# Scheduling edits across a hybrid GLA / sliding-window / gated-DeltaNet trunk on one core

## The reference, cut to what matters

```
x <- LN(ALPHA * x + even_mixer(x))     # GLA heads and sliding-window attention, one output projection
x <- LN(ALPHA * x + swiglu(x))         # 1024 -> 2816 -> 1024
x <- LN(ALPHA * x + gated_delta(x))    # conv(4) + SiLU on q, k, v; chunks of 64; inverse of (I + A)
x <- LN(ALPHA * x + swiglu(x))
GLA:   attn = where(causal, q_g @ k_g.T, 0) per chunk of 64; o = attn @ v + q_g @ state
delta: tmat = inverse(I + tril(kb @ k.T * gam, -1)); u = tmat @ vb; w = tmat @ (kb * exp(decay))
       v_new = u - w @ state; o = qd @ state + (q @ k.T * gam) @ v_new
       out = rms_norm(o) * norm_g * silu(gate)
```

## Time and profile before

| | us |
|---|---|
| median of 3 runs (1284.8 to 1287.28) | 1285.05 |
| the profiled execution | 1283.91 |
| its span, first to last instruction | 1282.1 |
| TensorE busy | 1250.3 (98%) |
| GpSimd busy | 598.9 (47%) |
| VectorE busy | 462.7 (36%) |
| ScalarE busy | 432.9 (34%) |

### The profile page before, as it was taken

The page is one execution under the profiler, slowest core; times in us unless marked ns, Lnnn a source line. Parts: engine busy times, 40 slices in busy tenths (PEclk is TensorE's granted clock), DMA queues, the critical chain, the costliest instruction groups (busy, mean ns, idle before and its releaser), DMA issues.

```text
span 1282.1 us, 16970 instructions
## 1 busy us (share of the span) xinstructions
PE 1250.3 (98%) x7104; PEld 1027.5 (80%) x7104; DVE 462.7 (36%) x763; ACT 432.9 (34%) x600; POOL 598.9 (47%) x286
## 2 busy tenths in 40 slices
PE   9999999999999999998999999999999999999997
PEld 7878877888888888886777878887788888888885
DVE  5548945211111000115687955553521101010105
ACT  4174623322222221224453355452422222221111
POOL 4241243964444443445743346364595444435341
PEclk9999999999999999999999999999999999999999
DMA  9321032333333233231344342022233333324221
GB/s 305 99 67 66 1 115 84 99 99 99 98 99 99 83 121 125 99 96 49 98 110 124 99 100 92 26 67 99 66 99 99 99 99 99 99 82 134 80 99 65
DMA packets 109375, 122.98 MB, mean 96 GB/s; under 512 B 22386, under 2 KB 84148, under 8 KB 109300
## 3 DMA queue, kind: packets, MB, share of 16 engines
q1 hardware_dynamic: 101828, 118.59, 29.4%
q10 hardware_dynamic: 7472, 3.31, 1.0%
HBM read 117.96 MB, written 3.70 MB: 95 GB/s over the span
## 4 chain that ended last, share of the span: by engine, by line
PE 86%; DVE 7%; POOL 3%; issue 3%; DVEq 1%; ACT 1%; ACTq 0%; POOLq 0%
PE bank L1562 26%; PE bank L1563 26%; PE bank L1564 26%; PE bank L1893 3%; POOL w_lo L638 2%; DVE f_ab L1083 1%; DVE KH L1355 1%; DVE OO L1333 1%; DVE SS L1331 1%; PE bank L1608 1%; DVEq L435 1%; PE bank L1721 0%; PE bank L1845 0%; DVE x_tm L1106 0%; PE bank L1782 0%
## 5 line engine op out<-in xcount | busy, mean ns | idle before, releaser
L638 POOL TENSOR_TENSOR w_lo<-w_raw,w_hi 128x1024 fp32r<-128x1024 f32 (+1 forms) x200 | 470.0, 2374 | 495.3 <-ACT w_hi L768 495.3
L1562 PE MATMUL bank<-x_hi,w_hi 128*128 128x512 f32 x928 | 364.3, 393 | 7.5 <-DVE f_ab L1083 4.0
L1564 PE MATMUL bank<-x_hi,w_lo 128*128 128x512 f32 x928 | 361.7, 390 | 0.0
L1563 PE MATMUL bank<-x_lo,w_hi 128*128 128x512 f32 x928 | 361.6, 390 | 0.0
L768 ACT ACTIVATE w_hi<-w_raw 128x1024 fp32r<-128x1024 f32 (+1 forms) x200 | 196.3, 1031 | 218.3 <-issue 167.3
L1562 PEld LDWEIGHTS bank<-x_hi,w_hi 128*128 128x128 f32 x928 | 174.6, 188 | 46.9 <-issue 8.4
L1564 PEld LDWEIGHTS bank<-x_hi,w_lo 128*128 128x128 f32 x928 | 174.5, 188 | 36.6
L1563 PEld LDWEIGHTS bank<-x_lo,w_hi 128*128 128x128 f32 x928 | 174.5, 188 | 35.4
L1150 DVE TENSOR_TENSOR f_ab<-bank,f_ab 128x512 f32<-128x512 f32 x44 | 30.4, 691 | 368.9 <-PE bank L1564 368.9
L1563 PE MATMUL bank<-w_lo,h_hi 128*128 128x512 f32 x352 | 140.4, 399 | 0.0
L1562 PE MATMUL bank<-w_hi,h_hi 128*128 128x512 f32 x352 | 138.7, 394 | 0.0
(11 more groups left out here) (270 smaller groups left out, 1179.5 us busy)
## 6 DMA issues: line engine op xcount, KB each, us to landing
w_raw<-ffn_w_gate_dram SPq DMA_DIRECT2D x22, 1024.0 KB, 5.3
w_raw<-ffn_w_up_dram SPq DMA_DIRECT2D x22, 1024.0 KB, 5.3
w_raw<-ffn_w_down_dram SPq DMA_DIRECT2D x20, 1024.0 KB, 5.0
w_raw<-od_w_in_dram SPq DMA_DIRECT2D x16, 1024.0 KB, 5.9
w_raw<-ev_w_in_dram SPq DMA_DIRECT2D x8, 1024.0 KB, 5.9
w_raw<-ev_w_out_dram SPq DMA_DIRECT2D x4, 1024.0 KB, 5.1
w_raw<-od_w_out_dram SPq DMA_DIRECT2D x4, 1024.0 KB, 5.1
x_fm<-x_fm_dram SPq DMA_DIRECT2D x8, 256.0 KB, 6.7
```

Of the source, the lines that this page charges most:

```text
L638: pool.tensor_tensor(w_lo[:, b % 2, c], w_raw[:, b % 2, c], w_hi[:, b % 2, c].bitcast(F32), ALU.subtract).then_inc(w_lo_ready, 1)
L1562: pe.matmul(out_ap, st[0], mv_[0], start=start, stop=False)
L1563: pe.matmul(out_ap, st[0], mv_[1], start=False, stop=False)
L1564: return pe.matmul(out_ap, st[1], mv_[0], start=False, stop=stop)
```

## The change

The masked GLA products are done by 64 x 64 chunk blocks instead of 128 x 128. Tail and last fillers are reordered by halves of k, and ("mix", 0, 0, 2) becomes a filler. LayerNorm's normalisation is written in two halves, each with its own z_norm count; GpSimd waits for all of them before it subtracts the first half of the next weight block, which now stands ahead of its low parts of x. fm_block with fresh does the two products with x_hi before it waits for x_lo. Bank rings restart in other places and orders. The inverse blocks lie in DRAM as two whole arrays, written by whole rows and read by two DMAs in place of one. The copy of ba_fm moves from VectorE to ScalarE, and ScalarE's rounding of the first og blocks moves ahead of two SiLUs. In the chunk loop qk stands between the small product and the small blocks, and filler place 0 ahead of vTM. The last tile's scale and gate are one VectorE instruction a head. Left out below: the shapes of g_at and upto (64 columns instead of 128) and three waits on blocks_landed, 128 instead of 64 a tile.

```diff
@@ -78,8 +78,7 @@
...
     i = np.arange(P)
-    same = (i[:, None] // CH) == (i[None, :] // CH)
-    upto = (same & (i[:, None] <= i[None, :])).astype(np.float32)
+    upto = (i[:, None] % CH <= np.arange(CH)[None, :]).astype(np.float32)
@@ -164,8 +163,10 @@
...
+EVEN_FILLERS = [[("gr", t)] for t in range(NT)]
 TAIL_FILLERS = {0: [("mix", 0, 0, 0), ("mix", 0, 0, 1)], 1: [("mix", 1, 0, 2)]}
-FILLED = set(FILLERS.values()) | set(TAIL_FILLERS[0]) | set(TAIL_FILLERS[1])
+LAST_FILLERS = {0: [("mix", 0, 0, 2)], 1: []}
+FILLED = set(FILLERS.values()) | set(TAIL_FILLERS[0] + TAIL_FILLERS[1] + LAST_FILLERS[0])
@@ -189,11 +190,12 @@
...
     for t in tiles:
-        u += [("score", t, 0), ("score", t, 1), ("kd", t), ("gr", t), ("gattn", t), ("gstate", t, 0), ("gout", t),
-              ("gstate", t, 1), ("probT", t, 0), ("probT", t, 1), ("sout", t)]
+        u += [("score", t, 0), ("score", t, 1), ("kd", t)] + EVEN_FILLERS[t]
+        u += [("gattn", t), ("gstate", t, 0), ("gout", t), ("gstate", t, 1), ("probT", t, 0), ("probT", t, 1)]
...
             u += [("oT", 0, t - 1, 0), ("oT", 0, t - 1, 1)]
-    u += TAIL_FILLERS[0] + [("oT", 0, NT - 1, 0), ("oT", 0, NT - 1, 1)]
+        u += [("sout", t)]
+    u += TAIL_FILLERS[0] + [("oT", 0, NT - 1, 0), ("oT", 0, NT - 1, 1)] + LAST_FILLERS[0]
@@ -220,9 +222,9 @@
...
         if t == 0:
-            u += filler(-1) + gram + both("kTM", "vTM") + filler(0) + both("qk") + filler(1) + m1 + filler(2) + ds
+            u += filler(-1) + gram + both("kTM") + filler(0) + both("vTM", "qk") + filler(1) + m1 + filler(2) + ds
         else:
-            u += gram + both("kTM", "vTM") + m1 + ds + both("qk") + filler(1) + both("kS")
+            u += gram + both("kTM", "vTM") + m1 + both("qk") + ds + filler(1) + both("kS")
@@ -235,12 +237,15 @@
...
     for key in u:
-        if key == ("conv", CONV_ORDER[0]):
+        if key == ("ba_fm",):
...
         elif key == FILLERS[0, -1]:
-            ring, turn = [0, 1, 2, 3, 6, 7, 4, 5], 0
+            ring, turn = [0, 6, 7, 1, 2, 3, 4, 5], 0
+        elif key == TAIL_FILLERS[1][0]:
+            free = [slots[k][0] for k in (("ds", NT - 1, 64), ("oT", 1, NT - 2, 0), ("oT", 1, NT - 2, 1))]
+            ring, turn = free + [b for b in ring if b not in free], 0
@@ -401,7 +406,7 @@
...
         dec32_dram = nc.dram_tensor("dec_rows32_out", (P // SB, TH, SB), F32).ap()
-        t_dram = nc.dram_tensor("t_blocks", (P, SB, 2, SB), F32).ap()
+        t_dram = nc.dram_tensor("t_blocks", (2, P, SB, SB), F32).ap()
@@ -596,9 +601,9 @@
...
             sp.wait_ge(s["t_blk_ready"], 1)
-            sp.dma_start(t_dram[:, :, 1, :], t_blkT).then_inc(s["t_blk_out"], 16)
+            sp.dma_start(t_dram[1, :, :, :], t_blkT).then_inc(s["t_blk_out"], 16)
             sp.wait_ge(s["t_blk_ready"], 2)
-            sp.dma_start(t_dram[:, :, 0, :], t_blk).then_inc(s["t_blk_out"], 16)
+            sp.dma_start(t_dram[0, :, :, :], t_blk).then_inc(s["t_blk_out"], 16)
@@ -607,8 +612,9 @@
...
                 for q in range(P // SB):
-                    src = t_dram[q * SB + t * GDN_H:q * SB + (t + 1) * GDN_H, :, :, :].rearrange("h i a c -> i h a c")
-                    sp.dma_start(blocks_in[q * SB:(q + 1) * SB, :, :, :], src).then_inc(s["blocks_landed"], 16)
+                    for a in range(2):
+                        src = t_dram[a, q * SB + t * GDN_H:q * SB + (t + 1) * GDN_H, :, :].rearrange("h i c -> i h c")
+                        sp.dma_start(blocks_in[q * SB:(q + 1) * SB, :, a, :], src).then_inc(s["blocks_landed"], 16)
@@ -632,8 +638,10 @@
...
         def _(pool):
-            def split_lo(b):
+            def split_lo(b, part=(0, 1)):
                 for i, c in enumerate(pieces(b)):
+                    if i not in part:
+                        continue
@@ -718,18 +726,18 @@
...
                             split_lo(first_block[name] + 1)
-                gate_output(NT - 1)
...
                     continue
-                split_lo(b)
+                split_lo(b, (1,) if b - 1 in turned else (0, 1))
...
                 if b in turned:
+                    pool.wait_ge(s["z_norm"], 2 * NT * turned[b])
+                    split_lo(b + 1, (0,))
@@ -878,8 +886,10 @@
...
                     act.activation(s_p[:, g, :], s_p[:, g, :], ACT.Exp).then_inc(s["s_prob"], 1)
-                full(act, ("gr", t))
-                take(act.activation(g_r[:, t, :], bank(("gr", t))[:, :], ACT.Silu), ("gr", t))
+                for key in EVEN_FILLERS[t]:
+                    if key[0] == "gr":
+                        full(act, key)
+                        take(act.activation(g_r[:, key[1], :], bank(key)[:, :], ACT.Silu), key)
@@ -923,6 +933,11 @@
...
                                scale=convw[:, 9 * KD + n:9 * KD + n + 1]).then_inc(s["conv_raw"], 1)
+                if i == 1:
+                    full(act, ("ba_fm",))
+                    take(act.activation(ba_fm[:, :], bank(("ba_fm",))[:, :], ACT.Copy), ("ba_fm",))
+                if i == len(CONV_ORDER) - 1:
+                    split_to(first_block[("og", 0)] + 1)
@@ -973,7 +988,6 @@
...
                     act.activation(decay32, decay32, ACT.Exp).then_inc(s["exp32"], 1)
-            split_to(first_block[("og", 0)] + 1)
@@ -1111,8 +1125,10 @@
...
                         return
-                    dve.tensor_scalar(x_tm[:, t, :], x_tm[:, t, :], mv[:, t, 0:1], rstd[:, t:t + 1],
-                                      ALU.subtract, ALU.mult).then_inc(s["z_norm"], 1)
+                    for h in range(2):
+                        c = slice(h * 512, (h + 1) * 512)
+                        dve.tensor_scalar(x_tm[:, t, c], x_tm[:, t, c], mv[:, t, 0:1], rstd[:, t:t + 1],
+                                          ALU.subtract, ALU.mult).then_inc(s["z_norm"], 1)
@@ -1250,8 +1266,11 @@
...
                 full(dve, ("gattn", t))
-                take(dve.copy_predicated(g_at[:, :, :], over_heads(upto[:, :].bitcast(I32), GH), k4(("gattn", t))),
-                     ("gattn", t))
+                take(dve.copy_predicated(g_at[:, :, :], over_heads(upto[:, :].bitcast(I32), GH),
+                                         bank(("gattn", t))[:, 0:GH * CH].rearrange("p (h n) -> p h n", h=GH)), ("gattn", t))
+                for key in EVEN_FILLERS[t]:
+                    if key[0] == "mix":
+                        add_sublayer(1, *key)
@@ -1299,6 +1318,8 @@
...
             round_o(0, NT - 1)
+            for key in LAST_FILLERS[0]:
+                add_sublayer(1, *key)
@@ -1357,9 +1378,6 @@
...
                 take(ins, key)
-                if i == 1:
-                    full(dve, ("ba_fm",))
-                    take(dve.tensor_copy(ba_fm[:, :], bank(("ba_fm",))[:, :]), ("ba_fm",))
@@ -1517,7 +1535,6 @@
...
                        .then_inc(s["kd_ready"], 1)
-                filler(t, 3)
@@ -1534,11 +1551,18 @@
...
             out_square_sum(NT - 1)
+            dve.wait_ge(s["or_ready"], NT)
+            link(dve.reciprocal(oms[:, :], oms[:, :]))
             for hg in range(2):
-                out_scale(NT - 1, hg)
+                dve.wait_ge(s["gate_ready"], OG_ORDER.index(("og", hg, NT - 1)) + 1)
+                for h in range(4 * hg, 4 * hg + 4):
+                    ins = dve.scalar_tensor_tensor(OO[:, h, :], OO[:, h, :], oms[:, h:h + 1],
+                                                   gate_s[:, NT - 1, h * P:(h + 1) * P], ALU.mult, ALU.mult)
+                ins.then_inc(s["o_odd"], 1)
+            filler(NT - 1, 3)
+            round_o(1, NT - 1)
...
                 add_sublayer(3, *key)
-            round_o(1, NT - 1)
@@ -1586,13 +1610,26 @@
...
                 steps = [(n, k) for n in range(len(keys)) for k in range(KD)]
+                for k in range(KD) if fresh is not None else ():
+                    weights_there(b, k)
+                    pe.wait_ge(s["x_hi_ready"], KD * fresh + k + 1)
+                    x = xcols(k, ALL)
+                    for n in range(len(keys)):
+                        ps = fill(keys[n]) if k == 0 else bank(keys[n])
+                        w = weights(b, k, n * P, P)
+                        pe.matmul(ps[:, :], w[0], x[0], start=k == 0, stop=False)
+                        pe.matmul(ps[:, :], w[1], x[0], start=False, stop=False)
+                    low_part_there(pe, fresh, k)
+                    for n in range(len(keys)):
+                        ins = pe.matmul(bank(keys[n])[:, :], weights(b, k, n * P, P)[0], x[1], start=False, stop=k == KD - 1)
+                        if k == KD - 1:
+                            done(ins, keys[n])
                 if fresh is not None:
-                    steps = [(n, k) for k in range(KD) for n in range(len(keys))]
+                    return
...
                         weights_there(b, k)
-                    if fresh is not None and n == 0:
-                        low_part_there(pe, fresh, k)
@@ -1664,6 +1701,8 @@
...
                               k == 0, k == KD - 1)
```

(62 more changed lines are left out.)

8 lines of the change are left out of this document (4 added, 4 removed).

## The result

The changed kernel took 1275.91 us (median of 4 executions, 1274.91 to 1277.72), the kernel before in the same session 1286.09 (4 executions, 1284.80 to 1287.28): ratio 0.9923, interval 0.9904 to 0.9941. It is faster, but by 9 to 10 us and not by 17.4, and 1275.91 lies above the upper end of the predicted range (1274). The profiled executions are 1283.91 before and 1274.91 after (span 1273.1): minus 9.0.

A forecast was written before the change was run, and what follows sets the result against it. The prediction took TensorE to bound the kernel, so only its work or gaps count. Six terms summed to -17.4 us: 1283.9 to 1266.5 by the profile, 1267.6 by the median, stated as 1267.5; eight in ten, 1262.5 to 1274.

The forecast's parts named there:

- ba_fm on ScalarE, smaller memsets and the ba ring lie under convolution matmuls: zero: Convolution phase: these three edits lie under convolution matmuls and change the time by zero.
- (b): Rival: VectorE becomes the limit at each turn, the odd turn and the even tiles; about 1273 us, chance 0.18.
- (c): Rival: in the even layer's g_at product the diagonal quarters do not overlap; +3.9, 1271.4 us, chance 0.06.
- (d): Rival: small block reads cost what small writes cost; the 3.2 wait returns as one for blocks; 1271 us, chance 0.08.
- (e): Rival: slower, as the inverse blocks' reads at each tile's start hold TensorE; 1289 us at 12 ns a piece, chance 0.05.
- Even layer, -5.4: Four token tiles: cheaper gattn, dearer g_at, waits covered by fillers, 0.4 given back for VectorE; -5.4 us.
- Turns to feed-forward, -1.6: Two turns to feed-forward: x_hi products first, earlier up-block weights, less a held low part; -0.8 us each, -1.6.
- Turn to the odd layer, -4.6: Turn to odd layer: first two convolution units get banks freed earlier, and the clock stays up; -4.6 us.
- Start of the chunk loop, -3.2: Chunk loop start: new bank order removes the 3.2 wait for KH, and inverse blocks land in time; -3.2 us.
- Chunk loop and tail, -2.6: Chunk loop: qk products cover three GA waits, -1.6 us; tail: cheaper last gate and fewer waits, -1.0.

The follow-up runs named there:

- e2: Kernel before, with only the restart of the six-bank ring moved from the first convolution unit to ba_fm, from bank 2; 1283.59 us, ratio 0.9977.
- e1: Changed kernel, with the six-bank ring at ba_fm starting from bank 2 instead of bank 0; 1267.54 us, ratio 0.9861.
- e4: e1 with the old layout of the inverse blocks (writes in 128-byte pieces, four reads a tile); 1268.05 us, ratio 0.9862.
- e3: e1 with gattn and g_at as four whole 128-column products again, and the wider masked copy; 1267.99 us, ratio 0.9864.
- e6: e1 with the old order of products behind each turn, three of a key, then three of the next; 1274.01 us, ratio 0.9916.
- e5: e1 with GpSimd's old order at the turns: no wait for the normalisation, no early half weight block; 1271.00 us, ratio 0.9887.
- e8: e1 with the normalisation of a token tile in one VectorE instruction instead of two halves; 1266.61 us, ratio 0.9850.
- e7: e1 with the old bank order at the start of the chunk loop; 1274.02 us, ratio 0.9906.
- e11: e8 with two more covers: last even tile's gate filler cut 4 and 4, tail filler five k-steps ahead of transposes; 1267.58 us, ratio 0.9864.

## Why the prediction was wrong

**The step that failed** is a half sentence: "ba_fm on ScalarE, smaller memsets and the ba ring lie under convolution matmuls: zero". The start of the ring was read for what it does at the turn, where it gained what was said (-4.15 for -4.6, and e2 alone -3.86), and for ba_fm itself. That it renumbers the banks of every unit up to the next start wasn't followed through. The convolution units' banks were taken as unchanged, while the 12th and the 13th now had the same one, and TensorE stood for all of VectorE's backlog between them. It cost 7.9 to 8.0 (the fifth stretch; e1), 5.42 as the wait and 12 x 0.2 = 2.4 for the clock. With this one number put right the kernel takes 1267.54; 1267.5 had been predicted. That it agrees so closely is luck: the other steps missed by up to 0.9 each way, and the misses cancel.

This also means that none of the rivals was the one that happened. (b) had 1273 for VectorE as the limit by other ways: at the turns, at the odd turn and in the even tiles; there the gains came within 0.9 of the forecast. (c) is refuted: the eight diagonal products take 1.02 where four whole ones take 0.99. By the rule of the Trainium skill quoted there (TensorEngine Tiling (Array Packing), Gotcha 1: PSUM Pressure) different row tiles cannot use one bank at once. The trace disagrees with it here: without an overlap the eight would have stood near the 2.2 that was the prediction's upper end. (d) is half true: the blocks' layout gained nothing (e4), but no wait returned either, as the blocks came 2.9 sooner with the old layout too. (e) is refuted: the reads land in 2.1 (median), by the DMA issues of the changed kernel from 730 to 770 us (count, KB each, median us to landing), which answer to the earlier trace rows:

```profile
t_blocks<-M SPq DMA_DIRECT2D x1, 512.0 KB, 6.4
blocks_in<-t_blocks SPq DMA_DIRECT2D x16, 32.0 KB, 2.1
```

**Point by point.**
- Even layer, -5.4: measured -6.18. gattn as said (0.99 to 0.61 in tile 0). The g_at product had been given +0.7 and costs +0.1. The pair nets 0.9 by "own" and 0.45 in the median (e3). That the terms' sum, -1.6 + 0.7, is 0.9 too is luck: g_at was priced 0.6 too high, and 0.4 of the rest was lost in waits and small steps.
- Turns to feed-forward, -1.6: measured -0.46 and -0.52, about -1.0. The x_hi wait of 0.96 and a low part held at 1.27 instead of the 0.98 allowed. Of its parts, the order of products is worth 1.35 a turn beside the held low part (e6), the early half block 0.9 to 1.2 (e5), the halved normalisation less than nothing (e8); I had 0.84, 0.2 less 0.3, and 0. e6's clock, 1.3 at two of three turns, was in no term.
- Turn to the odd layer, -4.6: measured -4.15, by the mechanism that was named.
- Start of the chunk loop, -3.2: measured -3.27, but of a wait that costs 5 when it is put back (e7), and with a wrong reason for the blocks: the write lands in 6.4 and not 3, and the reads' issue takes what it gained. They came in time because the copy ahead of the write was no longer held and the write landed sooner in any layout (e4), of which the prediction has nothing. The size is in part luck.
- Chunk loop and tail, -2.6: measured -1.75. The GA row is gone (1.6, three waits of 0.52), but each gave 0.4, since the qk products take 1.98 in their new place and took 1.81: in tile 2 it is 3.23 from the small product to the filler instead of 3.65. In tile 1 the weight load of that tile's second filler then stood 0.29 for GT, which takes 0.2 back. That is -1.0 for -1.6; the tail has -0.8 for its -1.0.

## What to carry to other kernels

When a ring of buffers is started at another place, write out the whole table of who has which buffer before and after, up to the next restart, and look for two neighbours with the same number: there the consumer's whole backlog is a wait. Price a wait of TensorE of some us with the slow products behind it, and not by the list of waits. And a single number off in a plan can eat half of a change that is otherwise as good as its parts; compare stretch by stretch, and the one that is out stands alone.

## What the runs showed of the hardware

- A gap of 3.19 us cost 3.2 in one execution and 5.0 and 5.9 in two others, with the granted clock at 0.50 for 3.6 and 5.6 us behind it (e7, e2). It fell also behind the waits of 5.42 and 7.62, behind two of three of 2.5 (e6), and in one profile behind one of 0.83 (e5), but not behind one of 1.69 (e2).
- A VectorE instruction between SBUF tiles that begins while a GpSimd one runs can last until that ends or some tenths longer: 0.19 became 2.42, 0.68 became 1.27, 1.25 became 2.67. Two that begin within 0.01 us of each other can go either way (0.19 in the changed kernel, 2.42 in e11).
- The same four loads of 128 KB landed in a median of 2.8 us in one execution and 5.2 in another, and the waits for GT go with it (0 in e1, 0.68 in e8, 1.51 in e6, 1.84 in e11).
- Eight 64-row by 64-column products with 128 columns each, two quarters of the array into the same bank, took 1.02 against 0.99 for four whole ones.
- Small pieces cost the write, more issues cost the reads: 512 KB in 128-byte pieces took 4.25 us on the queue and in rows 0.34, eight reads 4.46 and four 1.83 (e4, e1).
